# Layer 0's attention: the probabilities normalised by GpSimd, and the second of three copies of the turned probabilities made by VectorE

## The reference, cut to what matters

```python
def one_block(qblk):
    s = jnp.einsum('bqkgd,bskd->bkgqs', qblk, k, preferred_element_type=jnp.float32) * scale
    pr = jax.nn.softmax(s, axis=-1).astype(v.dtype)
    return jnp.einsum('bkgqs,bskd->bqkgd', pr, v)
```

## Time and profile before

| what | value |
|---|---|
| time, median of 3 runs | 3293.48 us (3293.22 to 3294.63) |
| span of the profiled execution | 3285.2 us |
| time beside the span (median less span) | 8.3 us |
| TensorE busy | 3111.3 us, 95% of the span |
| VectorE busy | 2259.3 us, 69% |
| ScalarE busy | 1887.4 us, 57% |
| GpSimd busy | 618.3 us, 19% |
| mean granted TensorE clock | 0.988 of full speed |

### The profile page before, as it was taken

The page is one execution under the profiler, slowest core; times in us unless marked ns, Lnnn a source line. Parts: engine busy times, 40 slices in busy tenths (PEclk is TensorE's granted clock), DMA queues, the critical chain, the costliest instruction groups (busy, mean ns, idle before and its releaser), DMA issues. The chain is left out here.

```text
span 3285.2 us, 55861 instructions
## 1 busy us (share of the span) xinstructions
PE 3111.3 (95%) x20268; PEld 2409.3 (73%) x20268; DVE 2259.3 (69%) x2853; ACT 1887.4 (57%) x2679; POOL 618.3 (19%) x479
## 2 busy tenths in 40 slices
PE   6999989989999999997999999999997999999999
PEld 4767878865777676765887888888885676767776
DVE  4777677557766666765686776867747666766666
ACT  3556848425665666554375583846723666556564
POOL 1200010001223322222111111021100222232221
PEclk9999999999999999998999999999998999999999
DMA  7230000449888888877010100100145888888885
GB/s 236 87 132 21 1 23 1 155 170 377 293 303 286 296 299 298 287 252 233 7 43 8 42 8 9 36 8 23 52 161 220 294 300 299 287 284 309 291 297 154
DMA packets 214175, 565.42 MB, mean 172 GB/s; under 512 B 33699, under 2 KB 71272, under 8 KB 213736
## 3 DMA queue, kind: packets, MB, share of 16 engines
q1 hardware_dynamic: 203614, 529.21, 44.6%
q0 software_dynamic: 9472, 33.57, 4.2%
q10 hardware_dynamic: 906, 0.23, 0.0%
HBM read 524.00 MB, written 38.94 MB: 171 GB/s over the span
## 5 line engine op out<-in xcount | busy, mean ns | idle before, releaser
L2188 DVE TENSOR_TENSOR moe_lo<-moe_raw,moeg_hi 128x2048 fp32r<-128x2048 f32 x384 | 882.8, 2327 | 289.3 <-ACT moeg_hi L2185 153.9
L2185 ACT CAST moeg_hi<-moe_raw 128x2048 fp32r<-128x2048 f32 x384 | 729.0, 1911 | 439.4 <-PE psum L2591 320.9
L1170 PE MATMUL psum<-attn_w_hi,attn_hs 128*128 128x512 f32 (+2 forms) x1424 | 368.3, 342 | 15.8 <-DVE attn_hs L1558 10.6
L1691 DVE TENSOR_REDUCE attn_neg_max<-psum 128x1 f32<-128x1280 f32 (+1 forms) x216 | 292.6, 1354 | 80.0 <-PE psum L1297 77.0
L1297 PE MATMUL psum<-attn_ks,attn_qst 128*128 128x512 f32 (+2 forms) x1200 | 310.7, 376 | 21.6 <-ACT attn_e L1467 19.5
L1467 ACT ACTIVATE attn_e<-psum,attn_neg_max 128x1280 f32<-128x1280 f32 (+1 forms) x216 | 264.6, 1226 | 60.9 <-DVE attn_neg_max L1691 54.8
L1170 PEld LDWEIGHTS psum<-attn_w_hi,attn_hs 128*128 128x128 f32 x1424 | 249.1, 189 | 47.8 <-DVE attn_hs L1558 11.8
L2591 PE MATMUL psum<-moe_lo,moeh_x_hi 128*128 128x512 f32 x960 | 262.0, 395 | 0.0
L2591 PE MATMUL psum<-moeg_hi,moeh_x_hi 128*128 128x512 f32 x960 | 261.6, 394 | 0.0
L2591 PE MATMUL psum<-moeg_hi,moeh_x_lo 128*128 128x512 f32 x960 | 260.6, 393 | 0.0
L1170 PE MATMUL psum<-attn_w_lo,attn_hs 128*128 128x256 f32 (+2 forms) x712 | 240.1, 337 | 0.0
(11 more groups left out here) (360 smaller groups left out, 5389.7 us busy)
## 6 DMA issues: line engine op xcount, KB each, us to landing
moe_raw<-in_l_w_gate SPq DMA_DIRECT2D x256, 512.0 KB, 4.1
moe_raw<-in_l_w_up SPq DMA_DIRECT2D x256, 512.0 KB, 5.1
moe_raw<-in_l_w_down SPq DMA_DIRECT2D x128, 1024.0 KB, 6.1
ada_w<-in_l_ada_w SPq DMA_DIRECT2D x19, 1024.0 KB, 13.9
ada1h_w<-in_l_ada_w SPq DMA_DIRECT2D x9, 1024.0 KB, 10.7
lru_ada<-in_l_ada_w SPq DMA_DIRECT2D x8, 1024.0 KB, 7.7
lru_late<-in_l_ada_w SPq DMA_DIRECT2D x8, 1024.0 KB, 11.8
out_w<-in_l_w_out SPq DMA_DIRECT2D x16, 512.0 KB, 5.9
```

Source lines behind the costliest of these rows:

```text
L1170: last = pe.matmul(out, hs[t % 2][:, part, k, :], right, start=(i == 0 and n == 0), stop=(i == KB - 1 and n == 2))
L1691: dve.tensor_reduce(neg_max[:, n:n + 1], m.psum[:, score_at(n):score_at(n) + hi - lo], AX.X, ALU.max, negate=True).then_inc(s["maxed"], 1)
L2185: act.copy(mm.hi[slot % 4][:, :, :], mm.raw[slot][:, :, :]).then_inc(mm.s["hi_ready"], 1)
L2188: dve.tensor_tensor(mm.lo[slot][:, :, :], mm.raw[slot][:, :, :], mm.hi[slot % 4][:, :, :].bitcast(F32), ALU.subtract).then_inc(mm.s["lo_re ...
```

## The change

In layer 0 VectorE now only takes the reciprocal and tells GpSimd (`inverted`); GpSimd, which gets a loop over all 36 units behind its nine powers, multiplies the probabilities in place and tells TensorE (`mixed`). The second turn of each latent unit (columns 512 to 1023, `b == 4`) is copied to SBUF by VectorE (`copy_probs`, told by `probs_copied`) and no longer by ScalarE. VectorE makes that copy in step `u + 2`, after `split_queries` where there is one and before `maxima(u + 3)`. The waits of TensorE for free banks are counted anew: `next_bank` waits for `probs_copied` where the user before the last was such a second turn. Layer 1 keeps its instructions.

```diff
     turns_k = KT + 1
     TURNS = turns_k + 2 * NT + 3 * (units - per_tile) + per_tile + (0, 2)[l]
+    ncopied = (units - per_tile, 0)[l]
+    reads = TURNS - ncopied
+    on_vector = lambda u, b: l == 0 and b == 4 and u < ncopied
...
                     pool.tensor_tensor(m.rstd[:, 0:nz], m.ssq[:, 0:nz], m.neg_half[:, 0:nz], ALU.pow).then_inc(s["rstd"], 1)
+                if l == 0:
+                    for u in range(units):
+                        lo, hi, _ = key_span(u)
+                        probs = e[u % 3][:, 0:hi - lo]
+                        wait_value(m, pool, s["inverted"], j * units + (u + 1))
+                        pool.tensor_scalar(probs, probs, inv[:, u:u + 1], None, ALU.mult).then_inc(s["mixed"], 1)
...
-                def next_bank(output=None, last=None):
+                def next_bank(output=None, last=None, vector=None):
...
+                        elif what == "vector":
+                            pe.wait_ge(s["probs_copied"], j * ncopied + count)
                         else:
-                            pe.wait_ge(s["turn_read"], j * TURNS + count)
+                            pe.wait_ge(s["turn_read"], j * reads + count)
...
+                    elif vector is not None:
+                        uses.append(("vector", vector + 1))
...
                     for b in turn_parts(n, part):
-                        at = next_turn()
+                        at = next_bank(vector=u) if on_vector(u, b) else next_bank()
+                        turn[0] += 1
...
                     _, _, tiles = key_span(2 * v)
-                    pe.wait_ge(s["turn_read"], j * TURNS + probs_at[2 * v + 1])
+                    pe.wait_ge(s["turn_read"], j * reads + probs_at[2 * v + 1])
+                    if on_vector(2 * v + 1, 4):
+                        pe.wait_ge(s["probs_copied"], j * ncopied + (2 * v + 2))
...
-                        if l == 0:
+                        if on_vector(u, b):
+                            turn[0] += 1
+                            used[0] += 1
+                        elif l == 0:
                             read_turn(pt[(u // 2) % 2][:, b:b + n, u % 2, :], n * P,
                                       groups_of=("p (n t) -> p n t", dict(t=P)))
...
                     dve.wait_ge(s["expd"], j * nmaps + (n + maps))
-                    dve.reciprocal(inv[:, n:n + maps], sums[:, n:n + maps])
-                    lo, hi, _ = key_span(u)
-                    dve.drain()
                     if l == 0:
-                        probs = e[u % 3][:, 0:hi - lo]
-                        dve.tensor_scalar(probs, probs, inv[:, n:n + 1], None, ALU.mult).then_inc(s["mixed"], 1)
+                        dve.reciprocal(inv[:, n:n + 1], sums[:, n:n + 1]).then_inc(s["inverted"], 1)
                     else:
+                        dve.reciprocal(inv[:, n:n + maps], sums[:, n:n + maps])
+                        lo, hi, _ = key_span(u)
+                        dve.drain()
...
+                def copy_probs(u):
+                    turned, at = copy_of[u]
+                    if u >= 4 and u % 2 == 0:
+                        dve.wait_ge(s["pv_done"], j * nvalues + (u // 2 - 1))
+                    dve.wait_ge(s["turned"], j * TURNS + turned)
+                    dve.tensor_copy(pt[(u // 2) % 2][:, 4:8, u % 2, :],
+                                    m.psum[:, at:at + 4 * P].rearrange("p (n t) -> p n t", t=P)
+                                    ).then_inc(s["probs_copied"], 1)
...
                     if l == 0 and u % per_tile == 0 and u > 0 and u // per_tile + 1 < NT:
                         split_queries(u // per_tile + 1)
+                    if u - lag in copy_of:
+                        copy_probs(u - lag)
                     if u + 1 < units and not (l == 0 and u == 1):
                         maxima(u + 1, 0)
```

More of the change, by code:

```diff
@@ L1199, in group @@
             def group(j, last_group):
-                turn, uses, keys_at = [0], [], {}
-                def next_bank(output=None, last=None):
+                turn, read, uses, keys_at = [0], [0], [], {}
+                def next_bank(output=None, last=None, vector=None):
                     n = len(uses)
@@ L1213, in next_bank @@
                                 pe.wait_ge(s["v_copied"], j * NT + NT)
+                        elif what == "vector":
+                            pe.wait_ge(s["probs_copied"], j * ncopied + count)
                         else:
-                            pe.wait_ge(s["turn_read"], j * TURNS + count)
+                            pe.wait_ge(s["turn_read"], j * reads + count)
                     if last is not None:
                         uses.append(("last", last))
-                    else:
-                        uses.append(("output", output + 1) if output is not None else ("transpose", turn[0] + 1))
+                    elif vector is not None:
+                        uses.append(("vector", vector + 1))
+                    else:
+                        uses.append(("output", output + 1) if output is not None else ("transpose", read[0] + 1))
+                        if output is None:
+                            read[0] += 1
                     return turn_bank(n)
@@ L1229, in turn_keys @@
                     at = next_turn()
-                    keys_at[i] = turn[0]
+                    keys_at[i] = read[0]
                     for n in range(nk):
@@ L1236, in cache_keys @@
                 def cache_keys():
-                    pe.wait_ge(s["turn_read"], j * TURNS)
+                    pe.wait_ge(s["turn_read"], j * reads)
                     for i in range(PT_TILES):
@@ L1273, in stage_half @@
                     last.then_inc(s["turned"], 1)
-                    staged[qt, half] = turn[0]
+                    staged[qt, half] = read[0]
                 def stage(qt):
@@ L1284, in scores @@
                         if u % per_tile == 0:
-                            pe.wait_ge(s["turn_read"], j * TURNS + staged[u // per_tile, (1, which)[l]])
+                            pe.wait_ge(s["turn_read"], j * reads + staged[u // per_tile, (1, which)[l]])
                         if u == 0 and which == 0:
-                            pe.wait_ge(s["turn_read"], j * TURNS + keys_at[NT - 2 + PT_TILES])
+                            pe.wait_ge(s["turn_read"], j * reads + keys_at[NT - 2 + PT_TILES])
                             pe.wait_ge(s["z_read"], j * NT + NT - 1)
@@ L1290, in scores @@
                         if u == units - per_tile and which == 0:
-                            pe.wait_ge(s["turn_read"], j * TURNS + keys_at[NT - 1 + PT_TILES])
+                            pe.wait_ge(s["turn_read"], j * reads + keys_at[NT - 1 + PT_TILES])
                         if n >= 2:
@@ L1315, in turn_probs @@
                         last.then_inc(s["turned"], 1)
-                    probs_at[u] = turn[0]
+                    probs_at[u] = read[0]
                 probs_at = {}
@@ L1334, in values @@
                     _, _, tiles = key_span(u)
-                    pe.wait_ge(s["turn_read"], j * TURNS + probs_at[u])
+                    pe.wait_ge(s["turn_read"], j * reads + probs_at[u])
                     at = next_bank(output=u)
@@ L1646, in split_queries @@
                     dve.tensor_tensor(qq[:, :, 1, :], view, qq[:, :, 0, :], ALU.subtract).then_inc(s["q_split"], 1)
-                staged_at, out_bank, keys_at, last_at, count, used = {}, {}, {}, [], [0], [0]
+                staged_at, out_bank, keys_at, copy_of, last_at, count, used = {}, {}, {}, {}, [], [0], [0]
                 def count_keys(i):
@@ L1674, in count_probs @@
                 def count_probs(u, part):
-                    count[0] += len(turn_parts(len(key_span(u)[2]), part))
-                    used[0] += len(turn_parts(len(key_span(u)[2]), part))
+                    for b in turn_parts(len(key_span(u)[2]), part):
+                        count[0] += 1
+                        if on_vector(u, b):
+                            copy_of[u] = (count[0], turn_bank(used[0]))
+                        used[0] += 1
                 def count_values(u):
```

2 lines of the change are left out of this document (1 added, 1 removed).

## The result

| | before | changed |
|---|---|---|
| median | 3294.06 us (3293.22 to 3296.52, 4 runs) | 3373.09 us (3371.07 to 3373.82, 4 runs) |
| ratio | 1 | 1.0241, interval 1.0228 to 1.0254 |
| span of the profiled execution | 3285.2 us | 3371.6 us |
| mean granted clock | 0.988 | 0.977 |

The account below looks back on a forecast made before the run. TensorE was taken to bound the kernel. Pairs with `split_queries` 9.8, other pairs -1.4, turned queries 0.5 and group starts 2.2 sum to +11.1 us: 3293.5 to 3304.6 us, range 3293 to 3318.

Parts of the forecast that it names:

- The bound and the price of relief: Layer 0's unit loops: TensorE sets the pace, so relieving ScalarE gains zero, at most some 3 us.
- GpSimd's multiplication: Normalising 1280 columns on GpSimd in layer 0: 1.33 us, scaled from a cast, 2.99 from a two-input operation; hidden at 1.33.
- Rival B: GpSimd is slow: from 2.33 us on, two multiplications run into `split_queries` and its casts wait; 3329.6 us, 12%.
- step 28: First group, `split_tokens` also ahead of the copy: values 1.9 us late, a 0.94 us wait goes, 0.7 us net.
- The start of a group: Steps 0 to 3: GpSimd and `finish_tile` hold each other up, `maxima(3)` 1.1 us late per group, +2.2 us.
- step 4: The turned keys, not the values, use the second turn's bank there; same cost as other `split_queries` pairs, 0.7 us.
- VectorE's copy and its place: Copy of 0.69 us behind `split_queries`: TensorE stands 0.8 us before the values in pairs with `split_queries`.
- the second chain: Behind the copy, `maxima(17)` is 0.55 us later, delaying the exponential and ScalarE's first copy; counted as costing nothing more.
- `read_out`: Without VectorE's multiplication ahead, it starts 0.10 us sooner for TensorE's second turn of odd steps: 0.1 us gained per pair.
- The shared resource: VectorE and GpSimd share one SBUF port pair, the second blocked until the first ends; sum 2.2 us, without it -0.6.

Follow-up runs that it names:

- e4: The changed kernel with GpSimd copying the probabilities onto themselves in place of multiplying them, normalisation left out; 3308.53 us, ratio 1.0039.
- e7: The changed kernel with GpSimd copying in place of multiplying (normalisation left out) and `copy_probs` ahead of `split_queries`; 3303.78 us, ratio 1.0027.
- e9: The changed kernel with 5 idle products on TensorE ahead of the values in steps with `split_queries`; 3363.13 us, ratio 1.0206.
- e10: The kernel before, with `read_out` put between the reciprocal and the multiplication of the even unit; 3292.68 us, ratio 0.9998.
- e3: The changed kernel with `copy_probs` ahead of `split_queries` in VectorE's queue; 3337.21 us, ratio 1.0131.
- e5: The changed kernel with GpSimd multiplying even units only, VectorE the odd ones, and ScalarE making all copies; 3315.04 us, ratio 1.0063.
- e8: The changed kernel with GpSimd multiplying even units by 0.5 and only 640 columns of odd units by their reciprocal; 3324.83 us, one run.

## Why the prediction was wrong, point by point

*The bound and the price of relief.* Right as far as the runs go: with 38 us of ScalarE's work and VectorE's multiplication taken away, e4 and e7 are still no faster than before. No run takes that work away and adds nothing, so that its worth by itself is not measured. (TensorE's idle 0.47 in 50 us is 2.4 us over the two loops, not some 3, and VectorE had more than a quarter of its time free, 28%; nothing hangs on either.)

*GpSimd's multiplication.* This is the step that failed: "I take 1.33, since the multiplication has one tensor input as the cast has". It takes 3.52 us, more than the 2.99 that was named as the upper bound from the two-input row. The count of tensor inputs was the wrong thing to scale by: GpSimd's COPY does take 1.26 us for these 1280 columns, its multiplication 3.5 with either kind of scalar. That one number is most of the loss, as e4 shows from the other side: 3308.5 us with an operation of 1.26 us, 3373.1 with 3.52 and all else alike, 64.6 of the 79 us. Why GpSimd's multiplication has this rate no run here shows.

*Rival B* named the mechanism: from 2.33 us on, the two multiplications run into `split_queries`. It had 12%. It expected 3329.6 us at 2.99 us; at 3.52 its own working gives two multiplications to 356.1 on the clock of the earlier trace rows, 2.4 us of delay in each of 14 pairs, 33 us, the first unit 0.7 us late, 10 us, and its 3 us for the starts, about 3350 us. The slower values, which no term had, add 1.5 us in 14 pairs, 21 us; e9 shows them to be the clock in 11 of these. Together that is 3371 us, but that it comes so near to 3373 is in part luck: it puts 5.2 us (0.7 - 0.1 + 2.4 + 0.7 + 1.5) on two pairs everywhere. The trace's sizes, from the periods: 4.0 us in each of 11 pairs with `split_queries` (2.46 idle ahead of the values and 1.5 in them), 44 us; 0.72 in most of the others, where the even unit is late (0.57 us of idle behind L1159 in the timeline above), 9 us; 17 us in steps 0 to 5 of the two groups; and 10 us from step 28 on in the first group, where the held operation is a `split_tokens` of two SBUF inputs (3.20 us for 1.22) and the values take 4.54 and 4.53 us. That is the 81 us. So two pairs in the middle cost 4.7 us and not 5.2, and the end of the first group twice what two pairs cost elsewhere.

*The start of a group.* The term was 1.1 us, and 0.7 for step 4. In e4, at the predicted length, steps 0 to 5 are 1.5 and 1.9 us longer, and an operation of `finish_tile` takes 1.27 us for 0.22 beside GpSimd's copy: the sum of the two terms was right, though not each by itself (the period with step 4 is 0.3 us shorter than before). In the changed kernel the same steps are 8.5 and 8.7 us longer. Windows over them in the first group, before and then changed (columns as in the earlier trace rows), and the first turn:

```profile
277.69:299.69 22.00, 17.75 (x138) 14.13 (x136) 16.70 (x26) 16.82 (x31) 0.00 (x0) 1.00 0.20 41
```

```profile
278.62:309.08 30.46, 20.48 (x137) 16.43 (x136) 21.30 (x25) 14.21 (x26) 21.11 (x6) 0.89 0.14 29
```

```profile
284.50 1.24 PE L1326 MATMUL psum<-ident,attn_e 128*128 128x128 f32 x8 [2.98 <-POOL attn_e L1159]
284.50 3.51 DVE L1594 CAST attn_khl<-attn_kf 128x64 fp32r<-128x64 f32 x1
```

Before the first turn TensorE waits 2.98 us for GpSimd's first multiplication, a cast of `finish_tile` of 0.20 us takes 3.51, and the granted clock is 0.89 on average (0.83 in the second group) where it was 1.00. How the 8.5 us divide among these wasn't taken apart.

*VectorE's copy and its place.* Right: 0.69 us, and 0.81 us of TensorE's time for 0.8 in e4. The clock in step 28 was missed, though the sum had the values 1.9 us late there. And the second chain, through `maxima(17)`, was counted as nothing; it is worth nothing only while the first one stands, as e7 shows.

*`read_out`.* Right in sign: 0.05 to 0.07 us for 0.1 (e4, e10).

*The shared resource.* The prediction took from a row that GpSimd and VectorE hold each other up, and used it only at the start of a group, at 1.33 us. The changed kernel, e3 and e5 show it in the middle: the held operation ended 0.15, 0.14 and 0.67 us after GpSimd's, a cast in the first two and a multiplication in e5, wherever it began. This is the rule of the Trainium skill, "SBUF — State Buffer", section "Who interferes with whom": casts and `tensor_scalar` can run in a two-port mode, and then whoever comes second is blocked until the other ends. The trace agrees, with 2.73 us for a cast of 0.28; in which mode it ran no run shows. That section also says that a `tensor_reduce` never contends. L1715 takes 1.49 us beside GpSimd's multiplication as without it, but it reads from PSUM, as the copy L1740 does that isn't held either, so this case is no test of that. The rule had been read rightly; the length that it was applied to was wrong.

*The range.* 3318 left rival B out on purpose, at 12%, because one input was thought to settle the rate. An operation that no row shows, with rows of 1.33 and 2.99 us at its sides and a threshold of 2.33 between them, deserved more than that. At 3.52 us the operation turned out to lie outside both rows.

## What to carry to other kernels

Before work goes to another engine, find a row of the very operation there; if there is none, a copy or a cast is no stand-in for arithmetic, and the threshold at which its length begins to collide should be priced with a chance near the middle. Ask what of its neighbour's work it can hold up, and what stands queued behind that: here 3.5 us on GpSimd held a 0.28 us cast, the cast held a copy, and the copy a bank. And when an edit makes TensorE idle in the middle of its work, look at the granted clock behind the gap as well as at the gap: here it made 4.0 us of 2.5.

## What the runs showed of the hardware that was not expected

- GpSimd's multiplication by a scalar costs 2.56 ns per column of 128 partitions in float32 (3.52 us for 1280, 1.89 for 640), by a constant 3.44 us; its copy 1.26 us (e8, e4).
- A VectorE cast or `tensor_scalar` between SBUF tensors that starts beside a running GpSimd operation ends only after it: 2.73 us for 0.28, 2.74 for 0.89. An operation with two SBUF inputs is held as well (3.20 us for 1.22). VectorE's reads from PSUM were not, in these runs: 0.69 us for the copy, 1.49 for `maxima`.
- After 2.46 us of idle time TensorE's 40 value matmuls took 3.96 us at a mean granted clock of 0.59, part of the stretch at the lower level of 1.2 GHz, against 2.40 us at the full 2.4 GHz. Behind gaps of 0.81 us (e4) they took 2.40 us, behind one of 1.93 us (e4, step 28) 3.85, behind one of 2.24 us (e3, step 28) 2.40, and behind 0.15 us with 1.33 us shortly before (e4, step 32) 4.01.
